# Moving the transposes of the expert hidden activations from TensorE to VectorE in a two-block transformer kernel

## The chip, the cores and the metric

The kernel runs on one core of one Trainium2 chip. The metric is the device time of one execution in microseconds (us), lower is better. Everything is float32.

## The reference

The reference computes two blocks on 256 positions of width 1024: a first block (attention with 8 heads, pooling, a gated feed-forward with a causal convolution) and a second block of an even layer (forgetting and sliding-window attention, dense feed-forward) and an odd layer (sparse attention, then a mixture of 8 experts). The part that the change touches most is the last one. Each token picks 2 of 8 experts, each of width 1408:

```python
logits = t @ router_w + router_b            # 256 x 8, top 2, softmax of the two
out[token] += weight * ((silu(t @ w_gate[e]) * (t @ w_up[e])) @ w_down[e])
```

The condition vector `c` also makes modulation vectors (`silu(c) @ ada_w + ada_b`), which scale, shift and gate each layer. Their weights are large and are multiplied on VectorE.

## The kernel before

Activations lie with features on partitions, as `x[128, 8, 256]` and `h`. Weights come from memory as slots of 512 KB (128 x 1024 floats), issued by SyncE in one long stream into a ring of 24 slots, each issue waiting until TensorE has used what lay in its slot.

**Experts.** Each expert works on up to `CAP` = 96 gathered tokens, in `BLOCKS` = 3 blocks of 32. The 1408 hidden units are split over `QUADS` = 4 groups of `QF` = 352, and TensorE works in column tiles of 32: four matmuls with 32 output partitions each run side by side. One expert takes 33 slots: 16 for the first 256 units of each group (`up_wide`), 6 for the other 96 (`up_narrow`), 11 for the way down (`expert_down`). An execution has 8 passes here. Slots 24 to 32 of a pass lie outside the ring, in `side` and `arena`. One pass of TensorE (`expert_pass`, L1333) is: `up_wide` (L1250), `up_narrow` (L1272), `row_transposes` (the gathered tokens of the next expert, L1324), `hidden_transposes` (L1294), `expert_down` (L1307). Between them ScalarE computes silu (L1657) and VectorE multiplies with the up half (`hidden`, L2292), giving `mhid` with tokens on partitions. Three column chunks of it (128, 128, 96) are transposed by TensorE against the identity and copied out of PSUM by ScalarE (L1662, L1665, L1668) and VectorE (L2308) into `mhidT`.

In pass 0 `row_transposes` stands before the last part of the way down. It needs rows that come by this road: VectorE runs `shifted_rows` (L2208), `extra_passes` (L2213 to L2236) and `row_numbers` (L2244 to L2269), GpSimd then scatters the tokens to memory by these numbers (L628, four indirect DMAs) and reads the next expert's rows back (L631). In the later passes GpSimd stores the results (L637) and reads rows ahead (L641). After the last of those it gathers the results of seven experts back per token (L644, four indirect DMAs of 512 KB). The extra rows (128 read, 96 used) are part of L631 and L641.

**Ahead of the experts** (TensorE): the output projection of the odd layer (`out_units`, L666 and L786) with `router_block` (L816), `norm_sum` (L727), `token_chunks` (L1193, transposes of the 256 tokens), a broadcast of the shift vector by matmuls (L1202, `brow`), the ranks (L1210 to L1214), `gather` (L1220). VectorE follows with picks and routing.

**The modulation weights.** `ada_load` (L605, GpSimd) loads 1 MB units into two slots, each load waiting until VectorE has used the unit two before; `ada_unit` (L1728) is VectorE's two products. Where in VectorE's program each unit stands is written by hand: in `attend` of the first block (units 0 to 10) and after five of the eight `br` units (five more, L2018), and in `last_third` (L1940) after the projection of the odd layer began. There `rope` (L1795 to L1803) follows, whose first operation frees the PSUM bank for which TensorE's next unit waits.

## Time and profile before

| | |
|---|---|
| median of 3 runs | 1320.54 us (1317.74 to 1320.67) |
| profiled execution | 1319.2 us, span 1317.6 us |
| mean granted clock of TensorE | 0.992 |
| HBM traffic over the span | 279 GB/s |
| TensorE busy | 1275.1 us (97%) |
| VectorE, ScalarE, GpSimd busy | 48%, 22%, 5% |

The page gives busy time by engine, a strip of the span in 40 slices, the chain of work that ended last, and groups of instructions by source line. TensorE's busy time is modelled, so 97% doesn't say that it could go no faster; the chain and the waits say what ends last. The share of the DMA engines is by packet time and can come out slightly over 1. Windows are in us from the start of the span.

### The profile page before, as it was taken

The numbers are of one execution on the slowest core, as the hardware profiler recorded it, in microseconds if no ns is written. First come the engines' busy times: TensorE is split into PE (matmuls) and PEld (weight loads), VectorE is DVE, ScalarE is ACT, GpSimd is POOL, SyncE is SP. The second block draws the span as 40 slices with busy tenths as digits, with TensorE's granted clock in tenths as the row PEclk, the third lists the DMA queues.
The fourth block names the chain that finished last, engine by engine and source line by source line (L and its number), as shares of the span: only waits on it lengthen the run. The fifth ranks groups of instructions, "written<-read, shape, count | busy, mean of one in ns | idle before, by whom it ended". The sixth has DMA issues, their size and how long they took to land.

```text
span 1317.6 us, 27465 instructions
## 1 busy us (share of the span) xinstructions
PE 1275.1 (97%) x10876; PEld 967.6 (73%) x10876; DVE 635.6 (48%) x1602; ACT 292.7 (22%) x772; POOL 71.0 (5%) x126
## 2 busy tenths in 40 slices
PE   6999999999999999999999998999989999999997
PEld 4768888999999767799999986778555455445545
DVE  5465464888887625457676764762610000000003
ACT  4332203212112414520000031264211011101103
POOL 0100000000000000000000001000010000000020
PEclk9999999999999999999999998999999999999998
DMA  9999783677776662237767776402999999999990
GB/s 348 413 401 403 262 298 125 213 282 271 266 276 236 254 214 80 97 113 267 288 254 286 278 285 232 168 1 97 383 411 409 410 410 410 410 410 410 410 378 32
DMA packets 92391, 368.72 MB, mean 280 GB/s; under 512 B 10243, under 2 KB 10499, under 8 KB 83930
## 3 DMA queue, kind: packets, MB, share of 16 engines
q1 hardware_dynamic: 75026, 271.29, 54.6%
q0 software_dynamic: 17296, 96.50, 18.9%
q8 instruction: 46, 0.75, 0.2%
q14 instruction: 23, 0.19, 0.0%
HBM read 347.69 MB, written 20.05 MB: 279 GB/s over the span
## 4 chain that ended last, share of the span: by engine, by line
PE 88%; DVE 4%; DMA 3%; issue 2%; ACT 2%; SPq 1%; POOL 0%; ACTq 0%; DVEq 0%; POOLq 0%
PE banks L941 20%; PE banks L666 15%; PE banks L928 11%; PE banks L1265 11%; PE banks L1316 8%; PE banks L1287 4%; PE banks L691 4%; PE banks L786 2%; PE banks L1008 2%; PE banks L746 2%; PE banks L857 1%; PE banks L841 1%; DMA ring<-stream 1%; DMA side<-ada 1%; DVE side L1728 1%
## 5 line engine op out<-in xcount | busy, mean ns | idle before, releaser
L1728 DVE CUSTOM_DVE_ANT_0 side<-side 128x1024 f32<-128x1024 f32 x128 | 151.0, 1220 | 33.6 <-DMA side<-ada 33.4
L1265 PE MATMUL banks<-ring,arena 128*32 128x512 f32 x1536 | 166.3, 592 | 0.0
L928 PE MATMUL banks<-arena,ring 128*128 128x256 f32 x704 | 160.2, 380 | 0.0
L666 PE MATMUL banks<-h,ring 128*128 128x256 f32 x640 | 145.8, 386 | 6.4 <-DVE arena L1798 5.6
L2292 DVE TENSOR_TENSOR arena<-arena,banks 128x256 f32<-128x256 f32 (+1 forms) x48 | 14.7, 334 | 284.4 <-ACT arena L1657 284.4
L928 PEld LDWEIGHTS banks<-arena,ring 128*128 128x128 f32 x704 | 130.2, 190 | 17.2 <-issue 1.4
L666 PEld LDWEIGHTS banks<-h,ring 128*128 128x128 f32 x640 | 121.6, 192 | 28.8 <-DVE arena L1798 5.7
L1265 PEld LDWEIGHTS banks<-ring,arena 128*32 128x32 f32 x1536 | 50.0, 110 | 111.2 <-issue 110.1
L666 PE MATMUL banks<-arena,ring 128*128 128x256 f32 x384 | 84.6, 380 | 2.6 <-DVE arena L2013 2.1
L941 PEld LDWEIGHTS banks<-h,ring 128*128 128x128 f32 x672 | 81.5, 192 | 2.1
L666 PEld LDWEIGHTS banks<-arena,ring 128*128 128x128 f32 x384 | 72.5, 190 | 13.3 <-DVE arena L2013 2.9
L941 PE MATMUL banks<-arena 128*128 128x128 f32 x672 | 81.9, 275 | 0.0
L941 PE MATMUL banks<-arena,ring 128*128 128x128 f32 x672 | 81.9, 275 | 0.0
L941 PE MATMUL banks<-h,ring 128*128 128x128 f32 x672 | 81.8, 275 | 0.0
L941 PEld LDWEIGHTS banks<-arena 128*128 128x128 f32 x672 | 78.4, 192 | 0.0
L941 PEld LDWEIGHTS banks<-arena,ring 128*128 128x128 f32 x672 | 78.4, 192 | 0.0
L605 POOL DMA_DIRECT2D side<-ada x64 | 33.9, 529 | 698.1 <-DVE msum L1728 688.5
L1507 ACT ACTIVATE arena<-banks 128x128 f32<-128x128 f32 x42 | 11.6, 277 | 265.5 <-PE banks L941 265.5
L1287 PE MATMUL banks<-ring,arena 128*32 128x192 f32 x1536 | 64.1, 326 | 0.0
L1316 PE MATMUL banks<-side,arena 128*32 128x256 f32 x1152 | 63.8, 379 | 0.0
L1287 PEld LDWEIGHTS banks<-ring,arena 128*32 128x32 f32 x1536 | 50.3, 110 | 16.6 <-issue 4.9
L1657 ACT ACTIVATE arena<-banks 128x256 f32<-128x256 f32 (+1 forms) x48 | 13.5, 318 | 212.5 <-PE banks L1265 162.0
(333 smaller groups left out, 1587.1 us busy)
## 6 DMA issues: line engine op xcount, KB each, us to landing
ring<-stream SPq DMA_DIRECT2D x247, 512.0 KB, 5.5
ring<-experts SPq DMA_DIRECT2D x192, 512.0 KB, 15.7
side<-ada POOLq DMA_DIRECT2D x64, 1024.0 KB, 7.6
side<-experts SPq DMA_DIRECT2D x48, 512.0 KB, 17.2
arena<-experts SPq DMA_DIRECT2D x24, 512.0 KB, 16.7
yrows<-side POOLq DMA_DIRECT2D x1, 6144.0 KB, 32.6
hrows<-side POOLq DMA_DIRECT2D x1, 5632.0 KB, 17.8
logit<-hrows POOLq DMA_DIRECT2D x8, 512.0 KB, 7.1
```

The source lines that it names most:

```text
L605: pool.dma_start(ada_slot[:, v % 2, :], ada[bass.ds(v + 8 * i, 1)].rearrange("a p r n -> p (a r n)")).then_inc(ada_full[v % 2], 16)
L666: last = pe.matmul(bank(u, a, a + T), ring[:, s, (k0 + kc) * P:(k0 + kc + 1) * P], moving[:, kc, :], start=(kc == 0), stop=(kc == kn - 1))
L691: last = pe.matmul(bank(u, at, at + width), h[:, kc, tile * P:(tile + 1) * P], ring[:, s, (kc % per) * width:(kc % per + 1) * width], star ...
L746: ins = pe.matmul(banks[:, b, 0:RAW], ring[:, pos % RING, k * P:(k + 1) * P], raw[:, k, :], start=(k == 0), stop=(k == KC - 1))
L786: last = pe.matmul(bank(u, (c % 2) * T, (c % 2 + 1) * T), ring[:, u.pos % RING, k * P:(k + 1) * P], moving[:, k, :], start=(k == 0 and c % ...
L928: last = pe.matmul(banks[:, 4 + c // 2, (c % 2) * T:(c % 2 + 1) * T], ring[:, s, c * P:(c + 1) * P], hid[:, j % 2, :], start=False, stop=F ...
L941: last = pe.matmul(banks[:, b, at * P:(at + 1) * P], weights[:, k * P:(k + 1) * P], moving[:, k, :], start=(start and k == 0), stop=(stop ...
L1008: ins = pe.matmul(bank(u, (n % 2) * T, (n % 2 + 1) * T), ring[:, u.pos % RING, k * P:(k + 1) * P], h[:, k, :], start=(k == 0 and n % 2 == ...
L1265: ins = pe.matmul(banks[BLOCK * j:BLOCK * (j + 1), t, :], hg[:, k, BLOCK * t:BLOCK * (t + 1)], ring[:, m, (j % 2) * 512:(j % 2 + 1) * 512] ...
L1287: ins = pe.matmul(banks[BLOCK * j:BLOCK * (j + 1), BLOCKS + t, 0:2 * NARROW], hg[:, k, BLOCK * t:BLOCK * (t + 1)], flat[:, at:at + 2 * NAR ...
L1316: ins = pe.matmul(banks[BLOCK * q:BLOCK * (q + 1), 6 + t // 2, (t % 2) * T:(t % 2 + 1) * T], mhidT[:, c, t, BLOCK * j:BLOCK * (j + 1)], mo ...
L1728: dve.tensor_tensor_reduce(weights, weights, cond[:, 0 if layer0 else 1, :], 1.0, 0.0, ALU.mult, ALU.add, accum_out=msum[:, n:n + 1]).then ...
```

## The change

1. `hidden_transposes` and the four evacuations of its result are gone. VectorE transposes each piece of `mhid` itself, in 32 by 32 blocks within SBUF, right behind the product of the next block: six `dve.transpose` in a pass. A block transpose leaves feature 32j+i of quad q at partition 32q+i, so the rows of the down weights are laid out anew on the host: slot c holds features 32c to 32c+31 of the four groups, eleven slots. `expert_down` runs over these eleven with waits on each transpose.
2. In pass 0 the way down is no longer broken by `row_transposes`, which comes at its end.
3. `row_numbers` goes ahead of `extra_passes`. The shift is added to the token rows by GpSimd, from a row that it stores to memory and reads back broadcast much earlier; the broadcast by matmuls and its two copies are gone. L631 and L641 read 96 rows.
4. Before the experts: six router blocks ahead of the last output unit (four before), `token_chunks` 0 and 2 before `norm_sum`, then the last two router blocks, then 1 and 3.
5. Odd layer: `rope(5)` comes ahead of the three last modulation units, and one unit stands between each two of the next ropes.
6. First block: 13 units in `attend` and 3 in the `br` loop (11 and 5 before).

```diff
             def expert_down(p, first, last):
...
                     for t in range(BLOCKS):
+                        if c == 0:
+                            pe.wait_ge(s_hidT, HIDS * p + t + 1)
+                        if c == WIDE // BLOCK:
+                            pe.wait_ge(s_hidT, HIDS * p + BLOCKS + t + 1)
                         for q in range(QUADS):
...
-                                            mhidT[:, c, t, BLOCK * j:BLOCK * (j + 1)], moe_slot(m)[:, T * q:T * (q + 1)],
+                                            mhidT[:, t, BLOCK * c:BLOCK * (c + 1)], moe_slot(m)[:, T * q:T * (q + 1)],
...
-                pe.wait_ge(s_hid, HIDS * p + 5)
-                hidden_transposes(0, 4)
-                pe.wait_ge(s_hid, HIDS * p + 6)
-                hidden_transposes(1, 5)
-                hidden_transposes(2, 3)
...
+                expert_down(p, WIDE // BLOCK, DOWN)
                 if first:
                     pick_transposes(1, 4)
                     row_transposes(p)
...
                 def hidden(s, at, w):
+                    for t in range(BLOCKS + 1):
...
+                        if t:
+                            dve.wait_ge(s_hid, n)
+                            dve.transpose(mhidT[:, t - 1, at:at + w], mhid[:, t - 1, at:at + w]).then_inc(s_hidT, 1)
...
                 if first:
-                    shifted_rows()
+                    slot_numbers()
+                    row_numbers()
                     extra_passes()
-                    row_numbers()
                     last_choice()
+                    dve.wait_ge(consts_set, 6)
```

GpSimd:

```diff
+            pool.dma_start(shift_row.rearrange("(p c) -> p c", p=P), mod[:, third, at:at + 8]).then_inc(nought_out, 16)
+            pool.wait_ge(nought_out, 16)
+            pool.dma_start(brow, shift_row.rearrange("(o n) -> o n", o=1).broadcast_to([P, D])).then_inc(nought_out, 16)
...
+            pool.wait_ge(s_gather, 2)
+            for tile in range(2):
+                rows = htok[:, tile, :].rearrange("t (c p) -> t c p", c=KC)
+                pool.tensor_tensor(rows, rows, brow.rearrange("t (p c) -> t c p", c=KC), ALU.add).then_inc(consts_set, 1)
+            pool.wait_ge(consts_set, 6)
+            pool.wait_ge(s_routed, 1)
...
-                pool.dma_start(hgtok, hrows[bass.ds((p + 1) * CAP, P), :]).then_inc(rows_in, 16)
+                pool.dma_start(hgtok[0:CAP, :], hrows[bass.ds((p + 1) * CAP, CAP), :]).then_inc(rows_in, 16)
```

The orders:

```diff
-            for t in range(4):
-                token_chunks(t)
...
+            token_chunks(0)
+            token_chunks(2)
+            norm_sum(5)
+            router_block(6)
+            router_block(7)
+            token_chunks(1)
+            token_chunks(3)
...
-            attend(first_heads, {0: units(0), 1: units(1), 2: units(2, 3), 3: units(4), 4: units(5), 5: units(6, 7),
-                                 6: [first_half_gate] + units(8), 7: units(9), 8: units(10)})
+            attend(first_heads, {0: units(0, 1), 1: units(2), 2: units(3), 3: units(4, 5), 4: units(6), 5: units(7) + [first_half_gate],
+                                 6: units(8, 9), 7: units(10), 8: units(11, 12)})
...
-                if 1 <= c <= 5:
-                    ada_unit(2, 2 + c)
+                if c in (1, 3, 5):
+                    ada_unit(2, 5 + c // 2)
...
-            last_third(8, (5, 6, 7), "o_ada_b")
+            rope(5, ikT, ("ik", 0))
+            for c in range(3):
+                ada_unit(8, 5 + c)
+                rope(6 + c, iqT[:, c, :], ("iq", c))
+            last_third(8, (), "o_ada_b")
+            rope(9, iqT[:, 3, :], ("iq", 3))
```

## Rows read from the trace of the kernel before

**Rows 1.** The page: the span, and busy time by engine.
```profile
span 1317.6 us, 27465 instructions
PE 1275.1 (97%) x10876; PEld 967.6 (73%) x10876; DVE 635.6 (48%) x1602; ACT 292.7 (22%) x772; POOL 71.0 (5%) x126
```
**Rows 2.** Windows: busy us (instructions) by engine, TensorE's granted clock, DMA share, GB/s.
```profile
1120.00:1160.00 40.00, 40.00 (x589) 19.80 (x581) 2.87 (x8) 4.67 (x14) 2.79 (x5) 1.00 1.03 410
980.00:985.00 5.00, 3.18 (x52) 2.15 (x56) 0.56 (x1) 0.49 (x1) 0.00 (x0) 1.00 1.03 410
805.00:810.00 5.00, 4.87 (x12) 3.93 (x13) 0.83 (x3) 0.00 (x0) 2.21 (x3) 0.54 0.59 223
```
**Rows 3.** The chain that ended last, one expert pass: start us, us, what.
```profile
1120.47 20.60 PE banks L1265 x192
1141.07 7.80 PE banks L1287 x192
1148.87 0.81 PE banks L1330 x8
1149.68 0.98 PE banks L1298 x9
1150.67 14.38 PE banks L1316 x264
```
**Rows 4.** Source view of L571, three single issues of the last pass.
```profile
L571 SPq DMA_DIRECT2D ring<-experts x1: 2362/2362/2362, 1247.4 to 1247.4; - x1
DMA to landing us min/median/max: 17.0/17.0/17.0
...
L571 SPq DMA_DIRECT2D side<-experts x1: 923/923/923, 1254.4 to 1254.4; - x1
DMA to landing us min/median/max: 18.9/18.9/18.9
...
L571 SPq DMA_DIRECT2D arena<-experts x1: 842/842/842, 1263.4 to 1263.4; - x1
DMA to landing us min/median/max: 21.3/21.3/21.3
```
**Rows 5.** Lines by form, 1120 to 1165: count, busy us, mean ns, idle before.
```profile
L2292 DVE TENSOR_TENSOR arena<-arena,banks 128x256 f32<-128x256 f32 x3 | 1.1, 417 | 35.4 <-ACT arena L1657 35.4
```
**Rows 6.** Timeline of pass 0: start us, us, instruction [idle before it, what ended that].
```profile
938.47 2.36 DVE L2208 TENSOR_TENSOR arena<-arena 128x1024 f32<-128x1024 f32 x2
942.78 1.01 DVE L2221 TENSOR_SCALAR logit<-logit 128x16 f32<-128x16 f32 x5
948.63 0.17 DVE L2244 TENSOR_SCALAR logit<-constants 128x8 f32<-128x8 f32 x1
957.42 1.03 POOL L628 DMA_INDIRECT hrows<-arena,logit  x1 [149.92 <-DVEq L2270]
981.82 0.88 PE L1330 MATMUL banks<-constants,logit 96*128 96x96 f32 x8 [3.27 <-DMA logit<-hrows]
```
**Rows 7.** The chain again, ahead of the experts.
```profile
925.70 3.46 PE banks L1193 x16
929.16 1.79 PE banks L1202 x16
```
**Rows 8.** Timeline, start of the odd layer.
```profile
798.52 0.59 PE L826 MATMUL banks<-arena,constants 128*128 128x256 f32 x2
804.17 0.95 POOL L621 MEMSET side<- 128x1024 f32 x1 [7.22 <-DVE mod L1747]
805.13 5.90 PE L666 MATMUL banks<-h,ring 128*128 128x256 f32 x16 [5.63 <-DVE arena L1798]
811.51 3.72 PE L666 MATMUL banks<-h,ring 128*128 128x256 f32 x16
```
**Rows 9.** Waits of TensorE, 84 to 230: us in total, times, longest.
```profile
PE banks L666 <- DVE arena L2013: 2.1, 2, 1.2
```
**Rows 10.** Timeline of GpSimd in the last pass.
```profile
1264.03 0.58 POOL L641 DMA_DIRECT2D logit<-hrows  x1 [5.61 <-DMA yrows<-arena]
1264.93 1.01 POOL L644 DMA_INDIRECT arena<-yrows,logit  x1 [0.33 <-issue]
```

More of the change, by code:

```diff
@@ L43 @@
 QF = WIDE + NARROW
-CHUNKS = ((0, P), (P, P), (WIDE, NARROW))
-DOWN_SLOT = (22, 26, 30)
+DOWN = QF // BLOCK
+DOWN_SLOT = 22
 MSLOTS = 33
@@ L385, in program @@
         scratch = nc.dram_tensor("bias_rows", (8 * P * 512,), F32, kind="Internal").ap()
+        shift_row = nc.dram_tensor("shift_row", (D,), F32, kind="Internal").ap()
         hrows = nc.dram_tensor("hrows", (NTAB * CAP + 64, D), F32, kind="Internal").ap()
@@ L802, in out_units @@
                     if r == 5 and c == 6:
-                        for k in range(4):
+                        for k in range(6):
                             router_block(k)
-                if r == 5:
-                    router_block(4)
-                    router_block(5)
-                    norm_sum(r)
-                    router_block(6)
-                    router_block(7)
             def router_block(k):
@@ L1194, in token_chunks @@
                 last.then_inc(aux_done, 1)
-            for t in range(4):
-                token_chunks(t)
-            third, at = norm_scale_source(5)[0]
-            pe.wait_ge(s_std, 6)
-            pe.wait_ge(s_route, 4)
-            for c in range(KC):
-                last = pe.matmul(banks[:, U["brow"].bank + c // 4, (c % 4) * P:(c % 4 + 1) * P],
-                                 mod[:, third, at + c:at + c + 1].broadcast_to([P, P]), ident,
-                                 start=(c % 4 == 0), stop=(c % 4 == 3), skip_group_check=True)
-            last.then_inc(aux_done, 1)
+            token_chunks(0)
[5 more added lines that the diff above has]
+            token_chunks(3)
             u = U["ranks"]
@@ L1292, in up_narrow @@
                                 ins.then_inc(slot_used[m], 1)
-            def hidden_transposes(c, b):
-                at, w = CHUNKS[c]
-                for t in range(BLOCKS):
-                    last = pe.transpose(banks[0:w, b, t * P:(t + 1) * P], mhid[:, t, at:at + w], ident)
-                last.then_inc(s_hidtr, 1)
             def pick_transposes(tile, b):
@@ L1305, in pick_transposes, with expert_down @@
                 last.then_inc(s_picktr, 1)
-            def expert_down(p, c):
-                count = 3 if c == 2 else QUADS
-                for j in range(count):
-                    m = DOWN_SLOT[c] + j
+            def expert_down(p, first, last):
+                for c in range(first, last):
+                    m = DOWN_SLOT + c
                     pe.wait_ge(slot_full[m], 16 * (before[m] + p + 1))
-                    final = c == 2 and j == count - 1
+                    final = c == DOWN - 1
                     for t in range(BLOCKS):
+                        if c == 0:
+                            pe.wait_ge(s_hidT, HIDS * p + t + 1)
+                        if c == WIDE // BLOCK:
+                            pe.wait_ge(s_hidT, HIDS * p + BLOCKS + t + 1)
                         for q in range(QUADS):
                             ins = pe.matmul(banks[BLOCK * q:BLOCK * (q + 1), 6 + t // 2, (t % 2) * T:(t % 2 + 1) * T],
-                                            mhidT[:, c, t, BLOCK * j:BLOCK * (j + 1)], moe_slot(m)[:, T * q:T * (q + 1)],
-                                            start=(c == 0 and j == 0 and t != 1), stop=final, skip_group_check=True)
+                                            mhidT[:, t, BLOCK * c:BLOCK * (c + 1)], moe_slot(m)[:, T * q:T * (q + 1)],
+                                            start=(c == 0 and t != 1), stop=final, skip_group_check=True)
                             if final:
@@ L1631, in _ @@
             act.wait_ge(s_rstd, 6)
-            for t in range(4):
+            for t in (0, 2, 1, 3):
                 u = U["htok", t]
@@ L1640, in _ @@
             act.activation(lg, lg, ACT.Exp).then_inc(s_gexp, 1)
-            act.wait_ge(*U["brow"].done)
-            for half in range(2):
-                act.activation(brow[:, half * 512:(half + 1) * 512], banks[:, U["brow"].bank + half, :], ACT.Copy).then_inc(s_h, 1)
             def gathered(half, b):
@@ L2069, in _ @@
             dve.tensor_reduce(bwsum, bw.rearrange("p c e -> p e c"), AX, ALU.add).then_inc(s_raw, 1)
-            rope(5, ikT, ("ik", 0))
-            for c in range(4):
-                rope(6 + c, iqT[:, c, :], ("iq", c))
             for m in range(8):
@@ L2202, in gathered, with slot_numbers @@
                 dve.tensor_copy(hg[:, 4 * half:4 * half + 4, :].rearrange("p a n -> p (a n)"), banks[:, b, 0:4 * CAP]).then_inc(s_hg_low, 1)
-            def shifted_rows():
-                dve.wait_ge(s_h, 46)
-                for tile in range(2):
-                    dve.tensor_tensor(htok[:, tile, :], htok[:, tile, :], brow, ALU.add)
-            def extra_passes():
+            def slot_numbers():
                 link(dve.tensor_copy(pre, over), s_route)
@@ L2219, in extra_passes @@
                 link(dve.tensor_tensor(slotno, a, over, ALU.mult), s_route)
+            def extra_passes():
                 for q in range(EXTRA):
@@ L2404, in _expert @@
     narrow = pair[..., WIDE:QF].reshape(KC, P, -1).transpose(1, 0, 2).reshape(P, -1, SLOT).transpose(1, 0, 2)
-    rows = down.reshape(QUADS, QF, D)
-    mixed = [np.concatenate([rows[a, WIDE:QF], rows[3, WIDE + BLOCK * a:WIDE + BLOCK * (a + 1)]]) for a in range(3)]
-    return np.concatenate([wide, narrow, rows[:, 0:P], rows[:, P:2 * P], np.stack(mixed)])
+    rows = down.reshape(QUADS, DOWN, BLOCK, D).transpose(1, 0, 2, 3).reshape(DOWN, P, D)
+    return np.concatenate([wide, narrow, rows])
 def _columns(v):
```

49 lines of the change are left out of this document (18 added, 31 removed).

## The prediction, written before the changed kernel ran

> **What bounds the kernel now.** I read the page first [rows 1]: a span of 1317.6 us in a profiled execution of 1319.2 us, so 1.6 us lie around the span; the median of the three runs is 1320.54 us, 1.3 us above the profiled one. TensorE is busy 97% of the span, which by itself says little. So I went to windows of the expert stage, about 937 to 1299 us [rows 2]: in 1120 to 1160 TensorE is busy throughout at the full clock, and the DMA engines are busy too, at 410 GB/s. Two resources are full at once. The chain of waits decides between them [rows 3]: a pass is 20.60 + 7.80 + 0.81 + 0.98 + 14.38 = 44.57 us of TensorE without a gap, the same in passes 1 to 7. So TensorE ends last, and each microsecond taken out of its pass counts, as long as the weights keep ahead.
>
> How far ahead they are is seen in the landings of the last pass [rows 4]. The 22nd slot (the last one of the way up) is issued at 1247.4 and lands 17.0 us later, at 1264.4. TensorE's last pass began at 1254.1 (1120.47 + 3 x 44.57); the narrow part begins 20.60 us later and its first block of tokens wants this slot 1.95 us into it (k = 6 of 8, a k step of one block being 7.80/24 = 0.325), at 1276.6. Lead: 12.2 us. The last slot lands at 1284.7 and is wanted at 1298.7 - 1.3 = 1297.4. Lead: 12.7 us. A slot of 0.524 MB at 410 GB/s takes 1.28 us; a pass moves 33 of them, 0.52 MB of token rows and 0.39 MB of results: 18.2 MB, 44.4 us. DMA is thus only 0.2 us a pass faster than TensorE is now, and its lead can't grow again once TensorE gets faster.
>
> **The change, part by part**, each against the span of 1317.6 us.
>
> *A, first block.* TensorE waits twice in the `br` loop for the product that frees its bank, 2.1 us in all [rows 9], because VectorE has a modulation unit (about 2.4 us, of two products) in five successive turns and waits for two of them. With three units in eight turns of 3.46 us each this goes: -2.1 us. The two units moved forward make VectorE wait longer inside `attend`, where TensorE has four gate units (14 us) between its needs. I found no place where it is caught. Bounds: 0 and -2.1; I take -2.1.
>
> *B, odd layer.* TensorE starts its unit at 805.13 after 5.63 us idle for VectorE's first rope product, which stands behind three modulation units; the unit then takes 5.90 us [rows 8] at a granted clock of 0.54 (near the 1.2 GHz level) [rows 2], the same unit later 3.72 us. With `rope(5)` in front, VectorE starts at once when the rotation of 798.52 is done, near 799.1, and TensorE at 799.6: -5.5 us, and -2.2 us as the clock has no gap to fall in. The small products that were behind the last unit now stand between the last rope and the index scores, +0.5 us. A unit and a rope (2.4 + 1.3 us) fit in a turn of TensorE (4.2 us). Sum -7.2 us; bounds -5 (the clock falls anyway, the third unit comes late) and -8. The clearing of the two buffers in memory (12 MB) starts some 14 us later, still done long before 934.
>
> *C, ahead of the experts.* The 16 transposes take 3.46 us, 0.22 each, and the broadcast 1.79 us [rows 7]; nine transposes of the same kind take 0.98 us, 0.11 each, in the experts [rows 3], so the first run at half clock. The broadcast goes, -1.8; eight transposes come earlier, before the thin matmuls of the norm after which the clock fell, -0.9. The router blocks only change place, though 0.85 us of them now lie ahead of the last output unit, and free its ring slot that much later. VectorE's picks come a little later than TensorE would want them, +0.4. Sum -2.3 us; bounds -1 and -3.5.
>
> *D, pass 0.* It lasts 49.9 us, 5.4 more than the others, of which 3.27 us is the wait for rows [rows 6]. With the rows at the end: 20.60 + 7.80 + 14.38 + 1.06 (picks) + 0.85 = 44.7, and 0.6 us for copies that were covered by the last part of the way down and now are not: 45.3 us, -4.6. For that the rows must be there by about 978. `row_numbers` is moved ahead of 5.85 us of `extra_passes` (942.78 to 948.63) and of the 2.36 us add, and all comes 2.3 us earlier: scatters start near 947 and not at 957.4, and the rows land near 971 instead of 981.8. Cover: 7 us. The add is now GpSimd's, between the gather (934.4) and 947. No row shows such an add there. Bounds: 0.95 us for each of two (its memset of the same size [rows 8]), and at the far end the 13 us that are free plus the 7 us of cover; I take 2 x 1.2 us, VectorE's own [rows 6], times two for a slower engine. It costs nothing on the path anywhere up to 20 us.
>
> The Trainium skill speaks against this move. Its page "GPSIMD Engine Reference" (the section on elementwise work side by side) gives 4497 ns for a float32 add of 2048 elements on GpSimd against 2293 ns on VectorE, and says that GpSimd shares SBUF interfaces with VectorE where that has two SBUF inputs. By it the two adds take an estimated 4.5 us; the sum wouldn't change.
>
> *E, passes 1 to 7.* The nine transposes go: 7 x 0.98 = -6.9 us. VectorE instead does three transposes of 128x256 and three of 128x96 in a pass. No row has one. Nearest is its product of the same size, 417 ns [rows 5]; from below 0, from above the point where it shows: the first three are wanted within 8.6 to 9.5 us of the end of the wide part, in which the products take 1.3 us, so up to 2.6 us each they are hidden. I take 0.42 us: VectorE is idle for over 35 us of a pass. Reading 96 rows for 128 saves 0.13 MB a pass, 0.32 us of DMA, nothing on TensorE.
>
> *F, what is late next.* At the last pass TensorE would be ahead by C + D + 6 x 0.98 = 12.8 us against now, more than the lead of 12.2. The 22nd slot moves too: +0.85 (C), and eight reads at 0.96 us fall ahead of it rather than seven at 1.28: -1.3. So 1264.0 against a need at 1263.8: level. But the gathers of results (L644), four times 0.52 MB, 5.1 us of DMA, start 0.9 us behind the last L641 [rows 10], and both hang on TensorE's pass 6, so they move by 12.8 us too, from 1264.9 to 1252.1. What they do to the slots is in [rows 4]: the 27th, issued at 1254.4, lands at 1273.3, 8.4 us after the first gather started, with only 1.3 us of delay over 1.28 us a slot and the row read; the last one carries all 5.1. The 22nd will be 11.9 us behind the first gather, and carries about 5: it lands at 1269, and TensorE stands still for 5 us of the last pass. From there, 5.85 + 0.81 + 14.38 = 21.0 us are left. The last slot then lands at 1284.7 + 0.85 - 2.6 = 1283, before its need at 1289. Bounds of this term: 0 (the gathers don't get ahead of queued slots) and 8 (the clock falls in the gap, as at 805, where a gap of 5.6 us was followed by 0.54; after the 3.3 us gap at 981 it stayed at 1.00 [rows 2]). I take +5.0.
>
> On this the page "DMA: Bandwidth & Descriptors" (arbitration) says that an engine takes turns between its queues packet by packet. By that alone the gathers would have half the bandwidth at once and the 27th slot 4 us of delay; the rows show 1.3, so I keep the rows' course.
>
> **Sum.** -2.1 - 7.2 - 2.3 - 4.6 - 6.9 + 5.0 = -18.1: a span of 1299.5, an execution of 1301.1, and with the 1.3 us by which the median stood above the profiled run 1302.4. Forecast: 1302 us.
>
> **Rivals.** *No new wait*: the weights stay ahead, F is 0 to 2, and the time is 1297. For it: half the bandwidth comes late in [rows 4]. Against: the leads are level even without the gathers. Chance 0.25. *More waiting*: the lead runs out a pass or two earlier (it is 0.2 us in pass 6 and 0.7 in pass 5 by the same count), or the clock falls in the gap, or A and B give only their near bounds: 1307. Chance 0.2. *Half of it isn't there*: the pieces outside the experts give nothing and F is 8: 1317.6 - 13.8 + 8 + 2.9 = 1315. Chance 0.04. *Slower*: the block transposes are the bound. Above 2.6 us for one of 128x256, each pass grows by three times the excess; from 3.3 us it eats the 18 us over eight passes. At 4 us: 8 x 4.2 = 34 us more, less the 5 of F, 1331 us. Against it: VectorE's rows of that size are all near 0.4 us. Chance 0.04.
>
> **How the numbers follow.** Forecast 0.47, no new wait 0.25, more waiting 0.2, half 0.04, slower 0.04. The forecast's own range is 1299 to 1305; 1295 to 1309 takes in the two next ones and leaves out about 1 in 6. About 0.3% (4 us) is what a measurement of this kernel can tell from no change. Faster 0.94, same 0.02, slower 0.04.
>
> **What would show it.** E: no TensorE transposes of `mhid`, a pass of 43.6 us, transposes of about 0.4 us on VectorE. D: pass 0 of about 45 us with no wait for rows. F: in the last pass a wait of TensorE at L1287 for a slot; or, if absent, the first rival. B: the unit after the first rotation starts near 0.5 us after it, at full clock. A: no wait on L2013. The prediction is wrong if the passes are still 44.5 us, or if the waits for slots start in pass 3 or 4, or if a transpose takes over 2.6 us.

## The result and the profile after

The changed kernel takes 1308.47 us (median of 4 runs, 1307.12 to 1309.64), the kernel before, run beside it, 1319.14 us. The ratio is 0.9926, 95% interval 0.9908 to 0.9944: faster by 0.56 to 0.92%. The forecast was 1302 us, with a range of 1299 to 1305. The sign and the list of parts were right, the size was not: 10.7 us came and 18.5 were forecast. The profiled execution took 1309.64 us with a span of 1308.0, against 1317.6 in [rows 1], so the two traces differ by 9.6 us.

The page of the changed kernel: span and busy time by engine.

```profile
span 1308.0 us, 27262 instructions
PE 1268.8 (97%) x10788; PEld 969.1 (74%) x10788; DVE 646.5 (49%) x1640; ACT 278.4 (21%) x730; POOL 77.4 (6%) x130
```

TensorE is still busy 97% of the span, as in [rows 1], and again this says little. What tells is the order of time. Timeline of TensorE in the odd layer, and the chain that ended last at the norm of the first block (start us, us, what):

```profile
800.00 0.59 PE L830 MATMUL banks<-arena,constants 128*128 128x256 f32 x2
800.64 3.72 PE L676 MATMUL banks<-h,ring 128*128 128x256 f32 x16
804.20 0.59 PE L830 MATMUL banks<-arena,constants 128*128 128x256 f32 x2
```
```profile
215.81 3.68 PE banks L756 x16
```

The unit that waited 5.63 us and ran at half clock [rows 8] now starts 0.05 us behind the rotation and takes 3.72 us. The piece at 215.81 started at 219.00 in the kernel before, so the first block gave 3.2 us, and the unit and the ropes of the odd layer 7.2 more. Then comes the stretch ahead of the experts, where the forecast begins to fail. Timeline of TensorE, changed kernel:

```profile
907.04 2.74 PE L820 MATMUL banks<-vectors,h 128*128 128x8 f32 x24
909.63 5.39 PE L676 MATMUL banks<-arena,ring 128*128 128x256 f32 x16
914.86 1.04 PE L1197 MATMUL banks<-constants,h 128*128 128x128 f32 x8
...
919.75 0.36 PE L1211 MATMUL banks<-logit,constants 128*128 128x8 f32 x2 [0.94 <-DVE logit L2134]
...
922.29 6.16 PE L1221 MATMUL banks<-arena 128*128 128x96 f32 x32 [0.91 <-DVE arena L2146]
928.38 20.81 PE L1265 MATMUL banks<-ring,arena 128*32 128x512 f32 x192
```

The transposes are cheap now (1.04 us for eight), and the broadcast is gone. But the last output unit took 5.39 us, where one at full clock takes 3.7, and the gather 6.16 us; in the kernel before the same gather took 3.78. The experts start at 928.38 and not at 936.60: 8.2 us earlier, of the 10.4 that had been gained. Windows of the granted clock (third column from the end), first two of the changed kernel, then two of the kernel before:

```profile
910.50:914.00 3.50, 3.50 (x11) 2.78 (x10) 0.00 (x0) 0.00 (x0) 0.00 (x0) 0.55 0.00 0
920.50:928.00 7.50, 6.59 (x35) 6.52 (x35) 4.03 (x16) 2.33 (x4) 0.00 (x0) 0.55 1.03 410
```
```profile
925.50:929.00 3.50, 3.50 (x19) 3.50 (x19) 1.88 (x12) 2.03 (x3) 0.00 (x0) 0.52 0.99 397
929.00:937.00 8.00, 7.09 (x63) 6.68 (x66) 4.26 (x17) 4.56 (x8) 0.00 (x0) 1.00 1.03 417
```

A mean of 0.55 over 7.5 us is 6.8 us at half clock (the 1.2 GHz level). The whole stretch, changed kernel and then kernel before:

```profile
910.00:935.00 25.00, 23.11 (x154) 17.02 (x156) 13.18 (x40) 6.37 (x11) 5.72 (x2) 0.80 0.77 299
```
```profile
910.00:935.00 25.00, 23.97 (x153) 22.50 (x152) 8.03 (x34) 10.11 (x19) 0.00 (x0) 0.93 0.67 249
```

The kernel before is at half clock for about 3.5 us, over its transposes. The changed one is so for about 10 us, over the output unit and the gather.

The expert stage. First TensorE in the last pass, then its waits from 900 us on (us in total, times, longest), then three issues of weights from the source view: the fifth slot of passes 5 and 6, and the 22nd of the last pass.

```profile
1238.05 20.78 PE L1265 MATMUL banks<-ring,arena 128*32 128x512 f32 x192
1258.65 1.52 PE L1287 MATMUL banks<-ring,arena 128*32 128x192 f32 x32
1261.79 0.53 PE L1287 MATMUL banks<-ring,arena 128*32 128x192 f32 x8 [1.62 <-DMA ring<-experts]
1264.43 0.53 PE L1287 MATMUL banks<-ring,arena 128*32 128x192 f32 x8 [2.11 <-DMA ring<-experts]
1266.36 8.82 PE L1287 MATMUL banks<-ring,arena 128*32 128x192 f32 x144 [1.40 <-DMA ring<-experts]
```
```profile
PE banks L1287 <- DMA ring<-experts: 5.1, 3, 2.1
PE banks L1211 <- DVE logit L2134: 0.9, 1, 0.9
PE banks L1221 <- DVE arena L2146: 0.9, 1, 0.9
PE banks L1287 <- issue: 0.9, 1, 0.9
```
```profile
L565 SPq DMA_DIRECT2D ring<-experts x1: 923/923/923, 1131.6 to 1131.6; - x1
...
DMA to landing us min/median/max: 15.5/15.5/15.5
...
L565 SPq DMA_DIRECT2D ring<-experts x1: 933/933/933, 1176.4 to 1176.4; - x1
...
DMA to landing us min/median/max: 15.7/15.7/15.7
...
L572 SPq DMA_DIRECT2D ring<-experts x1: 3305/3305/3305, 1242.4 to 1242.4; - x1
...
DMA to landing us min/median/max: 23.8/23.8/23.8
```

The last pass has the wait that term F names, in three pieces of 5.1 us in all: the 20th, 21st and 22nd slot come one behind the other. After it the clock is at half, and 144 products take 8.82 us where 7.80 x 144 / 192 = 5.85 are normal. The pass takes 52.3 us (1238.05 to 1290.31) against 44.7 before. The fifth slot lands at 1131.6 + 15.5 = 1147.1 and then at 1176.4 + 15.7 = 1192.1, 45.0 us apart; over all slots and passes the median is 44.8 to 44.9 us, where it was 44.4 in the kernel before. A pass of the weights moves fewer bytes and takes longer: this the forecast had the other way round. Windows of the changed kernel (columns as in [rows 2]), one pass, and the 3 us of one read of rows within it; the same 3 us in the kernel before (1134 to 1137) had 410:

```profile
1107.00:1147.00 40.00, 40.00 (x599) 19.46 (x591) 3.83 (x13) 3.05 (x9) 2.73 (x5) 1.00 1.03 402
1121.00:1124.00 3.00, 3.00 (x32) 0.91 (x28) 0.00 (x0) 0.00 (x0) 0.00 (x0) 1.00 1.04 313
```

The ledger, from the two traces in us: A -3.2, B -7.2, ahead of the experts +2.2, pass 0 -2.8 (49.94 to 47.12), the nine transposes -5.9 (4.93 in passes 1 to 6, 0.98 in the last), the last pass otherwise +8.55, the tail -1.2. Sum -9.6. These are single executions, one of each kernel.

### The profile page after: what moved, and what is told of

Same layout as the page of the kernel before. It is cut to its first block, busy times and chain, and to the rows that moved or that the text cites. A ratio compares the mean times of both kernels' runs of the same rounds, so it can differ in the third digit from the quotient of the medians.

```text
span 1308.0 us, 27262 instructions
## 1 busy us (share of the span) xinstructions
PE 1268.8 (97%) x10788; PEld 969.1 (74%) x10788; DVE 646.5 (49%) x1640; ACT 278.4 (21%) x730; POOL 77.4 (6%) x130
## 4 chain that ended last, share of the span: by engine, by line
PE 68%; SPq 23%; DMA 3%; issue 3%; DVE 2%; ACT 2%; ACTq 0%; DVEq 0%
PE banks L945 20%; SPq L565 19%; PE banks L676 17%; PE banks L932 11%; PE banks L701 4%; PE banks L796 2%; DMA ring<-experts 2%; PE banks L756 2%; SPq L561 2%; PE banks L1012 2%; SPq L572 2%; PE banks L1312 1%; PE banks L861 1%; PE banks L845 1%; DMA ring<-stream 1%
## 5 line engine op out<-in xcount | busy, mean ns | idle before, releaser
L1265 PEld LDWEIGHTS banks<-ring,arena 128*32 128x32 f32 x1536 | 51.3, 110 | 110.8 <-issue 109.7
L1287 PE MATMUL banks<-ring,arena 128*32 128x192 f32 x1536 | 68.9, 335 | 6.2 <-DMA ring<-experts 5.1
L1287 PEld LDWEIGHTS banks<-ring,arena 128*32 128x32 f32 x1536 | 55.1, 113 | 22.5 <-issue 10.7
```

The costliest lines, as they stand in the source:

```text
L1265: ins = pe.matmul(banks[BLOCK * j:BLOCK * (j + 1), t, :], hg[:, k, BLOCK * t:BLOCK * (t + 1)], ring[:, m, (j % 2) * 512:(j % 2 + 1) * 512] ...
L1287: ins = pe.matmul(banks[BLOCK * j:BLOCK * (j + 1), BLOCKS + t, 0:2 * NARROW], hg[:, k, BLOCK * t:BLOCK * (t + 1)], flat[:, at:at + 2 * NAR ...
```

## The experiments

Each time stands beside the kernel before in the same runs (1319.6 to 1321.3 us), with the ratio. Where a later kernel is put together from earlier edits, that is said and not shown again.

**The reads of rows: 128 rows again.**

```diff
-            pool.dma_start(hgtok[0:CAP, :], hrows[CAP:2 * CAP, :]).then_inc(rows_in, 16)
+            pool.dma_start(hgtok, hrows[CAP:CAP + P, :]).then_inc(rows_in, 16)
```

The same edit at L651.

> The changed kernel with the reads of token rows put back to 128 rows (L641, L651), nothing else. Theory R (the 96-row read is dearer for the DMA engines than the 128-row read): in the changed kernel the weights' first slot lands every 44.8 us, and during a 96-row read the engines fell from 410 to 280 to 290 GB/s for 2 us; with 128 rows the period is that of TensorE or 44.4 us, the last pass is 3 to 6 us shorter than 52.3 us, and the time is about 1304 to 1306 us against 1308.5. Rival S (the number of bytes counts): 0.13 MB more in each of 8 reads, 0.32 us each, the wait of the last pass grows by 2.5 us: about 1311 us.

Measured: 1306.11 us, ratio 0.99 (0.988 to 0.9919), span of the profile 1300.9. The weights' pass is back at 44.4 us, though more is moved, and the waits of the last pass are down from 5.1 to 2.3 us, the pass from 52.3 to 48.1. (The profiled execution, 1302.52 us, is the fastest of the four, 3.6 us below their median; its passes are read, not its sum.) The 3 us of the read (windows, all DMA traffic together):

```profile
1118.00:1121.00 3.00, 3.00 (x32) 0.91 (x28) 0.00 (x0) 0.00 (x0) 0.00 (x0) 1.00 1.02 407
```

Theory R holds. Its share in the median isn't resolved (the intervals of the two kernels overlap); the period and the rate are.

**112 rows.** As above, with `hgtok[0:112, :]`.

> The changed kernel with reads of 112 rows, between 96 and 128. It tells what makes the 96-row read dear. Theory P (a number of rows that isn't a multiple of 128 splits unevenly over partitions and engines, whatever its size): during the read the rate falls to 300 GB/s or less, and a pass of the weights takes 44.8 us or more. Rival (96 is special, its 6 rows of 4 KB for each of 16 engines): with 112 rows the rate stays at 400 and the period is 44.4 us.

Measured: 1308.21 us (one run), a pass of the weights 44.9 to 45.0 us, TensorE's waits in the last three passes, and in the read:

```profile
1117.00:1120.00 3.00, 3.00 (x32) 0.91 (x28) 0.00 (x0) 0.00 (x0) 0.00 (x0) 1.00 1.04 343
```

The rate is not under 300 as theory P put it, but the period is its 44.8 or more: 96 isn't special.

**96 rows in two reads, cut at 64, then cut at 32.**

```diff
-            pool.dma_start(hgtok[0:CAP, :], hrows[CAP:2 * CAP, :]).then_inc(rows_in, 16)
+            for a, b in ((0, 64), (64, CAP)):
+                pool.dma_start(hgtok[a:b, :], hrows[CAP + a:CAP + b, :]).then_inc(rows_in, 16)
```

The second kernel has `((0, 32), (32, CAP))`; both have the same at L651, and TensorE waits for 32 counts a pass.

> The changed kernel with each read of 96 rows made as two, of 64 and of 32 rows. Theory N (a read whose rows are a power of two runs at the full rate, 96 and 112 don't): the rate stays near 410 during the reads, a pass of the weights takes 44.1 us (0.96 and not 1.28 us for the rows), below the 44.4 us of the 128-row kernel, and the time is 1304 to 1306 us. Rival (whatever fills less than all 128 partitions is dear): the rate falls during both, the period is 44.8 us or more, 1308.5 us.

> The changed kernel with each read of 96 rows made as two, of 32 rows (partitions 0 to 31) and of 64 rows (partitions 32 to 95). Against the kernel whose reads were cut at 64 (0 to 63 and 64 to 95), only the place of the cut differs, not the bytes, the rows or the number of reads. That one had a pass of the weights of 45.2 to 45.4 us and 1313.5 us. Theory Q (partitions 0 to 63 are one half of the memory's write ports and 64 to 127 the other, so a read is as slow as the half that it fills most): the 64-row read now lies 32 rows in each half, the rate during the reads is above 310 GB/s, a pass takes 44.4 to 44.8 us and the time is near that of the changed kernel, 1306 to 1310 us. Rival (two reads cost more than one, wherever they are cut): 45.2 us and 1313 us again. The Trainium skill, page SBUF - State Buffer (section on the DMA port swizzle), has the map of partitions to ports from which theory Q is taken.

Measured: cut at 64, 1313.48 us (0.9941, 0.992 to 0.9961), a pass of the weights 45.0 to 45.7 us, eight waits for weights of 8.0 us; cut at 32, 1304.12 us (0.9887, 0.9871 to 0.9904), 44.4 to 44.5 us, no wait for weights in the last pass (43.7 us). The same bytes in the same number of reads, and 9.4 us between them; TensorE began the experts at nearly the same time in both profiles (930.48 and 931.53). Windows of 3 us over the reads, cut at 64, then cut at 32:

```profile
1122.00:1125.00 3.00, 3.00 (x32) 0.91 (x28) 0.00 (x0) 0.00 (x0) 0.00 (x0) 1.00 1.05 284
```
```profile
1124.00:1127.00 3.00, 3.00 (x32) 0.91 (x28) 0.00 (x0) 0.00 (x0) 0.00 (x0) 1.00 1.04 358
```

Theory N falls, and so does the rival that two reads are dear by themselves. Where the rows are cut is what counts. (The cut at 32 also has the smaller read first and the cut at 64 the larger; no run parts the two.) What a read costs can be estimated from the period: 33 slots at 1.28 us and 0.39 MB of results at 410 GB/s are 43.2 us, so 128 rows in one cost 1.2 us, 96 in one 1.7, 112 in one 1.8, 64 + 32 cut at 64 about 2.1, cut at 32 1.2 to 1.3 us. The Trainium skill, page "SBUF — State Buffer", section on the DMA port swizzle, has partitions 0 to 63 on 8 of 16 write ports and 64 to 127 on the other 8. By that rule the 64 rows cut at 32 lie half on either side, and those cut at 64 all on one; the runs agree in the direction. They agree in size for the cuts and for 128 rows, if a read costs what its fuller half holds: 32 + 32 rows for the cut at 32, 64 for 128 in one, 64 + 32 for the cut at 64. They don't for 96 and 112 rows in one, which would be no dearer than 128 (64 rows in the fuller half) and cost 0.5 to 0.6 us more. Why a single read of these is dear stays open.

**The gathers of results held back.**

```diff
+            pool.wait_ge(slot_full[21], 16 * (before21 + passes))
+            pool.dma_start(hgtok[CAP:CAP + 1, :], hrows[bass.ds(passes * CAP, 1), :]).then_inc(nought_out, 16)
             where = yrows.rearrange("e t s q n -> (e t s) (q n)")
```

> The changed kernel with the four gathers of results held until the 22nd slot of the last pass has landed (and one row of 4 KB read more, which carries the wait). Theory F of the prediction (the gathers run ahead of that slot and delay it by about 5 us): it lands 4 to 5 us earlier, the last pass takes 46 to 48 us instead of 52.3, the time is 4 to 6 us less, about 1303 us. Rival (the weights are late by themselves, since each pass of the DMA engines takes 44.8 us and not 43.6): the slot lands only 1 us earlier, and the time is within 2 us of 1308.5.

Measured: 1305.01 us, 0.9889 (0.9868 to 0.9911). The last pass takes 44.8 us with one wait of 0.75 us, and 0.3 and 1.3 us go in the two passes ahead of it. The 22nd slot landed 18.3 us after its issue and not 23.8.

> The changed kernel with the 128-row reads and the gathers held until the 22nd slot of the last pass has landed, both together (one row of 4 KB is read more, which carries the wait). If the two are separate causes of the last pass's 52.3 us, it takes 43.6 to 45 us, since 128 rows alone gave 48.1 and the held gathers alone 44.8 with waits in the two passes ahead of it: about 1302 us. If the held gathers only move the delay to the last eleven slots (which then carry all 5 us of it), the way down waits and the time is that of the 128-row kernel, 1306 us.

(From here on the row of 4 KB goes to `shift_row`.) Measured: 1300.07 us, 0.9856 (0.983 to 0.9883). Timelines of the last pass, TensorE and the first gather on GpSimd:

```profile
1237.36 20.78 PE L1269 MATMUL banks<-ring,arena 128*32 128x512 f32 x192
1257.96 7.98 PE L1291 MATMUL banks<-ring,arena 128*32 128x192 f32 x192
```
```profile
1260.28 1.00 POOL L658 DMA_INDIRECT arena<-yrows,logit  x1 [0.30 <-issue]
```

No wait, 43.7 us from 1237.36 to 1281.06, though the gathers start at 1260.28 and not at 1249.4: they are wanted only at the end of the pass. The last eleven slots carry them without a wait. So the two causes are separate, and together they are the whole 8.55 us: 5.1 of wait, 3.0 of half clock behind it, and some tenths.

**One part alone in the kernel before: the blocks.** The edits of term E in the kernel before. As the way down then has two calls and not three, pass 0 also takes its picks and its rows at its end, which is a part of D.

> The kernel before with one part of the change alone: VectorE's transposes in blocks of 32 by 32 and the eleven down slots of 32 rows; order, units, row numbers and the 128-row reads as before. By term E of the prediction passes 1 to 7 last 43.6 us and not 44.57, pass 0 also 0.98 less, and the lead of 12.2 us that the weights had in the last pass is used up only by 8 us: no wait for weights, 1319.1 - 7.9 = about 1311 us. Rival (the DMA engines hold each pass back: 44.4 us of transfers a pass): the last pass shows a wait for weights of some us and the time is 1314 or more.

Measured: 1309.72 us, 0.9929 (0.9907 to 0.995). Passes 2 to 6 take 43.59 us, the last 43.74, without a wait for weights: the 22nd slot landed at 1268.1, just when it was wanted (1245.71 + 20.60 + 1.95 = 1268.3). Pass 0 has 3.3 us less and pass 1 0.7 more. The forecast for this part holds, but the lead is gone, 12.2 us of it for 8.3 us of gain: the gathers started earlier with TensorE and took the rest.

**One part alone: the units.** The edits of A and B in the kernel before.

> The kernel before with the terms A and B of the prediction alone (modulation units and rope products rearranged in the first block and in the odd layer). In the changed kernel the traces show 3.2 and 7.2 us from these two. If nothing behind them takes it back (here the passes stay at 44.6 us, above the 44.4 us of the DMA engines): 1320 - 10.4 = 1309.6 us, with the experts 10.4 us earlier. Rival (the weights set the end, whatever is gained ahead of the experts): the lead in the last pass goes, and the time is 1313 or more.

Measured: 1308.91 us, 0.9916 (0.989 to 0.9942), span 10.2 us shorter; the experts start 11.1 us earlier, pass 0 takes 1.6 us more, the others 44.58 us as before. The 1.6 us go with half clock (971.7 to 975.1) behind the wait for rows. No pass waits for weights: in the last one the 22nd slot landed at 1253.2 and was wanted at 1267.1.

So one half alone gives 0.84% and the other 0.71%, in sum 1.55%. Both in one kernel, with C, the rest of D and the narrower reads, give 0.74%. With the two causes in the last pass mended it is 1.44%.

**Ahead of the experts.**

```diff
-                        for k in range(6):
+                        for k in range(4):
                             router_block(k)
...
+            router_block(4)
+            router_block(5)
             token_chunks(0)
```

> The changed kernel with two of the six router blocks put back behind the last output unit. Theory C (48 thin products in a row ahead of the output unit let the clock fall, and the unit then takes 5.3 instead of 3.6 us): with 32 of them the unit takes 3.6 us, its ring slot comes free 2 to 2.5 us earlier, the experts start 2 to 3 us earlier, and the weights with them, so that the whole is 2 to 3 us shorter: about 1306 us. Rival (the end is set by the DMA engines, whose work doesn't start earlier): the experts start earlier but the last pass waits as much longer, 1308.5 us. Rival (the clock falls anyway): no change anywhere.

Measured: 1307.19 us, 0.991 (0.9887 to 0.9933). The output unit takes 3.70 us, but half clock now holds from 917 to 927.5, the gather takes 6.97, and the experts start only 0.9 us earlier, 0.35 of which TensorE already had at the first router block. The kernel with 128-row reads has all six blocks ahead of the unit, and there the unit took 3.70 us as well; in the one with 128 rows and held gathers it took 5.39. Theory C as it was put falls: the blocks don't decide it.

The other order: all sixteen transposes behind the last router block, as in the kernel before, without the broadcast.

> The changed kernel with the order of TensorE ahead of the experts as in the kernel before (four router blocks, output unit, two blocks, norm sum, two blocks, the sixteen transposes), but without the broadcast of the shift. Theory C2 (with eight transposes moved up, TensorE waits twice for VectorE, 0.94 and 0.91 us, and the gather behind them runs at half clock, 6.2 to 7.0 us in three kernels with this order and 3.7 to 3.8 in the two with the old one): the transposes stand where the first wait was, the gather takes 3.8 us, and the experts start 1.5 to 2.5 us earlier than with the changed order, near 925.5 to 926.5 us, if what is upstream of it is as in the changed kernel. Rival (the broadcast kept the clock up, and the waits come back wherever the transposes stand): the gather takes 6 us or more and the experts start no earlier than 928. The whole: 1306 to 1307 us against 1308.5, if the weights follow.

Measured: 1306.37 us, 0.9905 (0.988 to 0.993). The transposes run at full clock, the first wait for VectorE is gone, and the experts start at 923.59, 4.8 us earlier. But the gather takes 5.41 us: the clock is at half from 919 to 923. With the units alone, where order and broadcast are those of the kernel before, it is at half from 920.5 to 924, and the gather takes 5.41 too. Theory C2 falls with its rival.

Single profiles are weak evidence here. The same instructions up to the experts are in eight of the sixteen kernels (the changed one; 128 and 112 rows; both cuts; held gathers; held with 128 rows; the adds on VectorE), and their experts start anywhere from 926.29 to 931.84. All sixteen profiles have at least one half-clock stretch between 910 and 935; in the kernel before and in the one with the blocks alone it lies on the transposes, in the others on the gather. Still, its length goes with the order. From the first router block to the first expert product, with the mean granted clock of 910 to 935:

| order | profiles | us | clock |
|---|---|---|---|
| before, with the broadcast | 3 | 19.12 to 19.16 | 0.93 |
| before, without it | 3 of 4 (the other) | 17.64 (21.75) | 0.93 (0.73) |
| changed, or changed with four router blocks ahead | 9 | 19.66 to 21.35 | 0.80 to 0.86 |

So dropping the broadcast gave 1.5 us in three profiles of four, and the changed order took 2.0 to 3.7 us against these three. Of the 4.8 us by which the experts start earlier here, 1.1 were there at the first router block. Some of the lead goes again later:

```profile
PE banks L1285 <- DMA ring<-experts: 6.9, 7, 2.1
```

Seven waits for weights, in passes 4 to 7 (44.04, 44.82, 44.78 and 52.25 us). At the start of pass 1 TensorE is 6.6 us ahead of the changed kernel (968.91 against 975.50), at the end of the last 3.9 us (1286.41 against 1290.31): with the weights at 44.8 us a pass, 2.7 us are waited for. The two medians aren't told apart.

**The adds on VectorE again.**

```diff
-                pool.tensor_tensor(rows, rows, brow.rearrange("t (p c) -> t c p", c=KC), ALU.add).then_inc(consts_set, 1)
+                        dve.tensor_tensor(rows, rows, brow.rearrange("t (p c) -> t c p", c=KC), ALU.add)
```

> The changed kernel with the two adds of the shift on VectorE again, ahead of the row numbers. Theory (GpSimd's adds, 5.7 us, held up VectorE, whose two copies of 8 columns took 2.3 and 2.8 us beside them and not 0.17): the adds take 2 x 1.2 us on VectorE, the small copies 0.2 us each, and the row numbers are done some 2.5 us earlier against the start of the experts. No change of the time beyond 1 us, as TensorE doesn't wait for rows either way. Rival (the copies were held up by something else, such as the gather's banks): they still take over 1 us.

Measured: 1309.68 us (one run), the experts and their end as in the changed kernel. Timelines: GpSimd and VectorE of the changed kernel, then VectorE of this one.

```profile
928.61 5.72 POOL L634 TENSOR_TENSOR arena<-arena 128x1024 f32<-128x1024 f32 x2 [112.02 <-PE banks L1221]
```
```profile
929.22 2.31 DVE L2175 COPY arena<-logit 128x8 f32<-128x8 f32 x1
931.57 2.79 DVE L2176 COPY arena<-logit 128x8 f32<-128x8 f32 x1
934.39 0.17 DVE L2175 COPY arena<-logit 128x8 f32<-128x8 f32 x1
```
```profile
928.99 0.18 DVE L2170 COPY arena<-logit 128x8 f32<-128x8 f32 x1
929.20 0.17 DVE L2171 COPY arena<-logit 128x8 f32<-128x8 f32 x1
930.04 4.05 DVE L2273 TENSOR_TENSOR arena<-arena 128x1024 f32<-128x1024 f32 x2
```

The copies are at 0.17 us again, so GpSimd's adds held VectorE up, and wholly: the first copy ends at 931.5, where the first add does (928.61 + 2.86), the second at 934.4, with the second add. (The Trainium skill, page "SBUF — State Buffer", says of GpSimd and a two-port operation of VectorE that one fully blocks the other; these times agree, though no trace shows in which mode the copies run.) The adds take 2.0 us each and not 1.2, as they read the shift with a stride now, and the first scatter comes 0.8 us earlier against the start of the experts, not 2.5. Moving the adds to GpSimd bought nothing: VectorE stood still for 4.8 us, where the adds would have kept it busy for 4.05.

**All of it.** Held gathers, the order of before, and 128-row reads; then the reads of 96 rows cut at 64; then cut at 32.

> The changed kernel with the 128-row reads, the held gathers and the old order of TensorE ahead of the experts: a version meant to beat both kernels. If the order gives 2 us at the start of the experts and the weights start as much earlier: about 1300 us. If the DMA engines set the end, it gives nothing beyond the kernel with two of the three, 1302 us, and a wait for weights shows in the last passes.

> The kernel with held gathers and the old order ahead of the experts (1297.9 us with 128-row reads), now with the 64 and 32 row reads. No wait for weights is left there, so cheaper reads gain nothing: 1297 to 1299 us. If the split reads are dear, a wait shows in the last pass: 1300 or more.

> The kernel with held gathers and the old order ahead of the experts, with the reads of 96 rows cut at row 32. With the cut at 64 the same kernel had passes of 45.2 us, waits for weights of 5.3 us and 1304.7 us; with 128 rows it had 43.6 us, no waits and 1297.9 us. Theory Q: the cut alone takes the waits away, passes of 43.6 us and 1296 to 1299 us. Rival (the gain of the cut in the kernel before this one was due to its later start of the experts): waits for weights of 2 us or more, 1301 or more.

Measured: 1297.91 us (0.9827, 0.9803 to 0.9851), 1304.66 us (0.988, 0.9852 to 0.9908) and 1298.00 us (0.9831, 0.9813 to 0.9849). Cut at 64, the passes from 4 on are held at 45.2 us and more by the weights. Cut at 32, TensorE in the last pass has one wait, and the pass takes 44.8 us:

```profile
1254.71 2.29 PE L1291 MATMUL banks<-ring,arena 128*32 128x192 f32 x48
1257.75 6.06 PE L1291 MATMUL banks<-ring,arena 128*32 128x192 f32 x144 [0.75 <-DMA ring<-experts]
```

The first of these profiles had half clock for 14 us ahead of the experts and took 1304.72 us, 6.8 us above its median; only its passes are read. The first and the third beat both kernels, by some 10 us against the changed one; with two of the three edits (1300.07 us) it isn't told apart from them. Theory Q holds at the early start too, but for a wait of 0.75 us.

## Why the prediction was wrong in size

*A and B* held: -2.1 forecast and -3.2 found, -7.2 and -7.2. Half of the other 1.1 us isn't A's: at the wait of L857 the changed kernel was 0.5 us ahead (119.17 against 119.71), and so was the kernel with the blocks alone (119.10), whose first block is that of before. The rest is open. B's -7.2 is in part luck. Its -2.2 rest on a clock that has no gap to fall in, and in seven of the fourteen profiles with this edit TensorE is at half clock some 15 us later, between 816 and 827, over the index scores and what follows them (window of the kernel with held gathers):

```profile
816.00:827.00 11.00, 10.52 (x38) 7.88 (x37) 9.40 (x32) 2.94 (x6) 1.12 (x2) 0.69 0.97 374
```

The first router block then starts at 908.3 to 910.8 and not at 906.0 to 907.6. The changed kernel's profile is among the seven without it; what decides it is open.

*C is the step that failed first*: -2.3 forecast, +2.2 found, outside its bounds (-1 and -3.5), and +0.5 at best in the other profiles of this order. Its parts came as put: the transposes take 0.13 us each, and the broadcast is gone. The forecast took the half clock of [rows 7] for a cost of the transposes that goes when they are moved. But there is half clock in this stretch in every order that was run, and it slows what comes to stand there. In the kernel before it was about 3.5 us, in the changed one about 10; if work at half clock takes twice its time, that is some 3.3 us of the 4.5 that C missed. The wait of 0.94 us at L1211, which the kernel before doesn't have, is the next part; the forecast put 0.4 us for such. Why the changed order has more half clock stays open.

*D*: -4.6 forecast, -2.8 found in this execution. With 128 rows, with held gathers and with both, pass 0 takes 45.33 us, the forecast's 45.3. The 1.8 us are a stop of 0.9 us in the narrow part that the list of waits gives to issue, and a slower run beside it; one other kernel has it (cut at 32, 47.15 us), most don't. The mechanism was right: no wait for rows. But its cover was smaller than forecast. Against the start of the experts the forecast has the scatters at 947 - 934.3 = 12.7 us (934.3 being 936.6 less the 2.3 of C) and the rows at 971 - 934.3 = 36.7; found are 945.9 - 928.4 = 17.5 and 969.7 - 928.4 = 41.3. These 4.8 us are what VectorE's two copies lost beside GpSimd's adds (2.31 + 2.79 less 2 x 0.17). The rows landed 4.3 us before the 973.95 at which TensorE took them, not 7. The adds took 5.7 us, where the forecast had 4.8, and 4.5 from the page "GPSIMD Engine Reference" of the Trainium skill. What was missed is what the same page says of the interface that GpSimd and VectorE share: the forecast took VectorE to run on beside it.

*E*: -6.9 forecast, -5.9 found. The four settled passes take 43.59 us (43.6 forecast), a transpose 0.42 us (0.42). Passes 1 and 2 are 0.6 and 0.4 us longer, in the narrow part, in nearly all kernels with the change and without a wait in the list; that stays open.

*F is the other step that failed*: +5.0 forecast, +8.55 found, past the bound of 8. The wait itself was right in size and place, 5.1 us at L1287, but for reasons that made up for each other. TensorE started the last pass at 1238.05, 6 us later than the forecast's terms have it (1254.02 - 2.1 - 7.2 - 2.3 - 4.6 - 5.9 = 1231.9), and the weights were as much slower. The wrong premise is that 96 rows for 128 save 0.32 us of DMA: they cost some 0.4 us more, eight times. A count of bytes can't show that, and [rows 2] had only 128-row reads. On how the gathers compete, the forecast kept the course of [rows 4] against the page of the Trainium skill "DMA: Bandwidth & Descriptors", by which the queues take turns. The rule was right, in the kernel before too, and the rows were read too short. Source view of L571 there, the 25th and the 30th slot of the last pass:

```profile
L571 SPq DMA_DIRECT2D side<-experts x1: 929/929/929, 1252.2 to 1252.2; - x1
DMA to landing us min/median/max: 16.0/16.0/16.0
...
L571 SPq DMA_DIRECT2D side<-experts x1: 3740/3740/3740, 1257.2 to 1257.2; - x1
DMA to landing us min/median/max: 23.8/23.8/23.8
```

They land at 1268.2 and 1281.0: five slots in 12.8 us, 2.56 us each and not 1.28. In the same time go the row read and the four gathers, five transfers of the same size, which land at 1271.1, 1273.7, 1276.3, 1278.8 and 1281.3. This begins 4.2 us after the issue of the row read (1264.03), which goes first. The 27th slot, at 1273.3, had met only the read and one gather, hence its delay of 1.3 us. In the changed kernel slots came 2.64 us apart (1261.79, 1264.43) while the gathers ran, the next one 1.93 (1266.36). So the +5.0 would have been much the same by that rule. The rest of F is the clock behind the wait, 3.0 us, which the forecast had as a bound and not in the value.

*The rivals*: no new wait (1297) needed DMA to stay ahead; with 128 rows and the gathers held it does, and the time is 1300. More waiting (1307) is what came, and one of its grounds, half clock in the gap, is in the trace; in this execution A and B gave no less than forecast. The slow transposes were nowhere near.

The sum of the misses: C 4.5, F 3.55, D 1.8, E 1.0, less 1.1 for A and 1.2 for the tail, is 8.5 us: the difference between the forecast's -18.1 and -9.6. The tail does the same work; its thin products of the norm took 1.95 us and not 2.66, at a higher clock.

## What to carry to other kernels

When TensorE's pass comes within 1% of what the DMA engines need for it, price every transfer by a row of its own shape, not by its bytes, and ask which later transfer the faster engine will release early. Here, holding back four gathers that nobody wants yet, and reading 128 rows or cutting 96 at row 32, are worth about 0.7% together, nearly as much again as the whole change. A stretch at half clock didn't go with the work that stood in it: price what moves there at half clock, and read more than one profile of it, as the same code had 7 to 10 us of it here.

## What the runs showed of the hardware

- During a read into fewer than 128 partitions the rate of all DMA traffic together falls: 313 GB/s over 3 us for 96 partitions, 343 for 112, 284 for 64 + 32 cut at 64, 358 cut at 32, 407 to 410 for 128.
- Reads and gathers of 0.52 MB from GpSimd's queue and weights of that size from SyncE's take turns: five slots came 2.56 us apart, 1.28 alone, beginning 4.2 us after the first issue on GpSimd.
- GpSimd's add of 128x1024 takes 2.9 us, and VectorE's copies of 128x8 take 2.3 to 2.8 us beside it, 0.17 alone. VectorE's add of that size takes 1.2 us with straight operands and 2.0 with one that is read with a stride.
- VectorE transposes 128x256 in blocks of 32 by 32 in 0.42 to 0.44 us and 128x96 in 0.26 us, as long as a product of that size takes.
- Each of the sixteen profiles has TensorE at half clock for 3.5 to 14 us between 910 and 935, whatever stood there: the same output unit took 3.70 or 5.39 us, the same gather 3.78 or 5.4 to 7.0. Ahead of it stand thin products (8 columns and 1 column) and, in most, short waits; no order of these that was run prevented it. Between 816 and 827, seven of the fourteen profiles with the same code there have it and seven don't.
